# First mixers of a deep fp32 network on one core: gate projections moved last, raw copies of them, stick-breaking on every turn, output projection begun inside the attention

## The reference

```
def _token_mixer(h, w_in, w_out):
    proj = h @ w_in
    ...
    rq, rk, rv, rg, dq, dk, dv, sq, sk, sv = jnp.split(proj, points, axis=-1)
    ...
    y_ret = _retention(_rotate(_split_heads(rq, RET_HEADS), ret_freq),
                       _rotate(_split_heads(rk, RET_HEADS), ret_freq),
                       _split_heads(rv, RET_HEADS), rg)
    y_dil = _merge_heads(_dilated_attention(_rotate(_split_heads(dq, DIL_HEADS), rope_freq),
                                            _rotate(_split_heads(dk, DIL_HEADS), rope_freq),
                                            _split_heads(dv, DIL_HEADS)))
    y_sb = _merge_heads(_stick_breaking(_split_heads(sq, SB_HEADS), _split_heads(sk, SB_HEADS),
                                        _split_heads(sv, SB_HEADS)))
    y = jnp.concatenate([y_ret, y_dil, y_sb], -1).astype(h.dtype)
    return y @ w_out
...
def _retention(q, k, v, g):
    ...
    o = (o - mu) * lax.rsqrt(var + GN_EPS)
    return jax.nn.silu(g.astype(jnp.float32)) * _merge_heads(o)
...
def _stick_breaking(q, k, v):
        ...
        z = jnp.einsum('bhqd,bhsd->bhqs', q_blk, kf)
        log_beta = jax.nn.log_sigmoid(z)
        log_keep = jnp.where(causal, jax.nn.log_sigmoid(-z), 0.0)
        between = lax.cumsum(log_keep, axis=3, reverse=True) - log_keep
        a = jnp.where(causal, jnp.exp(log_beta + between), 0.0)
        return jnp.einsum('bhqs,bhsd->bhqd', a, vf)
```

## Time and profile before

| | us |
|---|---|
| median of 3 runs (3520.35 to 3524.16) | 3522.71 |
| profiled execution, span | 3520.2 |
| PE busy | 3433.7 (98%) |
| DVE busy | 1894.9 (54%) |
| ACT busy | 1198.5 (34%) |
| POOL busy | 519.9 (15%) |

### The profile page before, as it was taken

How to read it: one execution, slowest core, us unless ns; L and a number is a source line. 1 busy time by engine, 2 the same in 40 slices (tenths; PEclk the granted TensorE clock), 3 DMA queues, 4 the chain that set the end, 5 groups by cost and what they waited for, 6 DMA issues and landing times. The chain is left out here.

```text
span 3520.2 us, 40510 instructions
## 1 busy us (share of the span) xinstructions
PE 3433.7 (98%) x16478; PEld 2789.2 (79%) x16478; DVE 1894.9 (54%) x3227; ACT 1198.5 (34%) x1646; POOL 519.9 (15%) x454
## 2 busy tenths in 40 slices
PE   8999999999999999999999999989999999999999
PEld 5888876688888888876788877757888888878887
DVE  5555753664556455744752346885643345564433
ACT  3222352442224222453442234445432222352221
POOL 1010231210012010231210021112011110211111
PEclk9999999999999999999999999979999999999999
DMA  6444221133442444211132212101222222322221
GB/s 264 178 180 179 92 77 60 49 144 144 168 144 108 155 156 161 93 58 48 63 142 96 96 66 84 60 13 61 73 96 96 96 96 99 108 73 96 96 96 72
DMA packets 53036, 372.53 MB, mean 106 GB/s; under 512 B 6001, under 2 KB 6129, under 8 KB 10098
## 3 DMA queue, kind: packets, MB, share of 16 engines
q1 hardware_dynamic: 52850, 369.94, 28.8%
HBM read 367.82 MB, written 2.10 MB: 105 GB/s over the span
## 5 line engine op out<-in xcount | busy, mean ns | idle before, releaser
L1487 PE MATMUL ps<-s_hh,s_wh 128*128 128x512 f32 x2552 | 1012.8, 397 | 18.8 <-POOL s_hl L2691 14.1
L1487 PE MATMUL ps<-s_hh,s_wl 128*128 128x512 f32 x2552 | 998.3, 391 | 0.0
L1487 PE MATMUL ps<-s_hl,s_wh 128*128 128x512 f32 x2552 | 998.0, 391 | 0.0
L2137 DVE TENSOR_TENSOR s_wl<-s_stage,s_wh 128x2048 fp32r<-128x2048 f32 (+1 forms) x276 | 623.5, 2259 | 635.3 <-ACT s_wh L1814 635.3
L1814 ACT ACTIVATE s_wh<-s_stage 128x2048 fp32r<-128x2048 f32 (+1 forms) x276 | 519.2, 1881 | 586.0 <-PE ps L1487 427.0
L1487 PEld LDWEIGHTS ps<-s_hh,s_wh 128*128 128x128 f32 x2552 | 481.7, 189 | 138.9 <-issue 34.9
L1487 PEld LDWEIGHTS ps<-s_hh,s_wl 128*128 128x128 f32 x2552 | 481.7, 189 | 102.7
L1487 PE MATMUL ps<-s_ah,s_wh 128*128 128x512 f32 x1408 | 561.9, 399 | 0.7 <-POOL s_al L2730 0.7
L1487 PEld LDWEIGHTS ps<-s_hl,s_wh 128*128 128x128 f32 x2552 | 482.5, 189 | 98.0 <-issue 0.7
L1487 PE MATMUL ps<-s_ah,s_wl 128*128 128x512 f32 x1408 | 550.1, 391 | 0.0
L1487 PE MATMUL ps<-s_al,s_wh 128*128 128x512 f32 x1408 | 549.5, 390 | 0.0
(11 more groups left out here) (502 smaller groups left out, 3614.7 us busy)
## 6 DMA issues: line engine op xcount, KB each, us to landing
s_stage<-in_w_ada SPq DMA_DIRECT2D x64, 1024.0 KB, 4.8
s_stage<-in_ffn_w_gate SPq DMA_DIRECT2D x44, 1024.0 KB, 4.8
s_stage<-in_ffn_w_up SPq DMA_DIRECT2D x44, 1024.0 KB, 4.8
s_stage<-in_ffn_down SPq DMA_DIRECT2D x32, 1024.0 KB, 4.8
s_stage<-in_w_up SPq DMA_DIRECT2D x32, 1024.0 KB, 4.7
s_stage<-in_down_m SPq DMA_DIRECT2D x32, 1024.0 KB, 4.7
s_stage<-in_w_in SPq DMA_DIRECT2D x24, 1024.0 KB, 4.8
s_stage<-in_ffn_down SPq DMA_DIRECT2D x16, 768.0 KB, 4.3
```

Of the source, the lines that this page charges most:

```text
L1487: return pe.matmul(out, lhs, rhs, start=start, stop=stop, skip_group_check=True)
L2137: ins = dve.tensor_tensor(m.wl(ws)[:, a:z], m.STAGE[:, j % NS, a:z], m.wh(ws)[:, a:z].bitcast(F32), ALU.subtract)
```

## The change

It moves work within both mixers and leaves every product as it was.

- **Gates last.** The gate chunks 4 and 5 are projected behind dv. Their 8 groups run beside the dilated units, which before ran alone. The last product of a pair of dilated heads waits (`hold`) until all four gates are projected.
- **Raw copies.** `m_gate` copies the gate from PSUM to `rg`. `m_silu` applies Silu in place later, when all four gates are copied and all sixteen dilated exponentials (`weighed`) are in ACT's list.
- **Stick-breaking on every turn.** `pace = 2` is gone and `depth` is 5. The four tiles of `rg`, free until the gates come, serve as further scratch (`xg`), and later those of `rq` and `rk` (`xr`) serve the dilated units.
- **Output projection.** The order is (6, 7, 4, 5, 0, 1, 2, 3). Tiles are split when they are there (`ready`, `parted`), the first group (tiles 6 and 7) is put among the dilated units, and what is left of these runs from `pipeline` inside `project_out`. `m_part` of the retention's tiles is called in `ret_norm`.
- **Smaller things.** The first w_out chunk takes no chunk of w_ada along, so these move by one place in the following stages; `m_center` waits for its own previous result; ACT has 8 table loads where it had 16.

```
+            if ready:
+                self.until(lambda: ready(ks[i]) and ready(ks[i + 1]))
...
-            ch = self.take(name, idx0 + c, ada=c == 0)
-            tiles = (self.feat2(ch, kt, x, ver, True, order=order) if per == 2 and c == 0 else
+            ch = self.take(name, idx0 + c, ada=c == 0 and not ready)
+            tiles = (self.feat2(ch, kt, x, ver, True, order=order, ready=ready) if per == 2 and c == 0 else
                      (self.feat(ch, kt, nc, t, x, ver) for t in range(per)))
             for t, (b, pid) in enumerate(tiles):
+                if extra:
+                    self.pipeline()
+                    self.tmp.ids = [i for i in self.tmp.ids if i not in extra]
+                    self.burst, self.depth, extra = 1, 6, ()
...
+            while len(gated) < 4 or len(weighed) < 16:
+                yield
             for h in range(4):
-                b = self.banks.take()
-                self.add("ret_out", l, h, y, b)
-                self.banks.free(b, ("ret.out", l, h))
-                yield
+                self.add("m_silu", l, h)
+            yield
+            for h in range(5):
+                if h < 4:
+                    b = self.banks.take()
+                    self.add("ret_out", l, h, y, b)
+                    self.banks.free(b, ("ret.out", l, h))
+                if h:
+                    self.add("m_part", l, h - 1, (h - 1) % 2, self.hv, self.hfree)
+                    parted.append(h - 1)
+                if h % 2:
+                    yield
...
-        def setpace(n):
-            self.pace = n
+        def used_up():
+            for i in used:
+                self.tmp.after[i] = [("ret.s", l, h, 3) for h in range(4)]
+            self.tmp.ids += used
+            self.burst, self.depth = 2, 9
             return True
...
-        for i in extra:
+        for i in extra + unused:
             self.tmp.after[i] = [free]
-        self.tmp.ids += extra
+        self.tmp.ids += extra + unused
         tproj(11, "sv", 0)
         self.bg.extend(sb_units())
-        self.pace = 2
+        self.depth = 5
         proj(0, "rq")
         proj(1, "rk")
         self.active += [roped("rq", "ret"), roped("rk", "ret")]
         tproj(2, "rv", 0)
         tproj(3, "rv", 256)
-        self.bg.append(lambda: setpace(1))
         self.bg.append(lambda: len(ropes) >= 2 and len(sb_done) == 2)
         self.bg.extend(ret_units())
+        self.tmp.ids = [i for i in self.tmp.ids if i not in unused]
+        proj(6, "dq")
+        proj(7, "dk")
+        self.active += [roped("dq", "dil"), roped("dk", "dil")]
+        tproj(8, "dv", 0)
+        self.hv += 1
+        self.bg.append(lambda: len(ropes) == 4 and len(out_done) == 4 and used_up())
+        self.bg.extend(dil_units())
         for c in range(2):
             ch = self.take("w_in", l * 12 + 4 + c, ada=False)
             for t in range(2):
+                n = 2 * c + t
                 b, pid = self.feat(ch, 8, 256, t, "h", hv, turn=False)
-                self.add("m_gate", l, 2 * c + t, pid, b)
-                self.banks.free(b, ("m.g", l, 2 * c + t))
+                self.until(lambda: ("xg", n) not in self.tmp.busy)
+                self.add("m_gate", l, n, pid, b, self.tmp.after[("xg", n)])
+                self.banks.free(b, ("m.raw", l, n))
+                self.hfree = ("proj", pid)
+                gated.append(n)
                 self.tick()
             self.release(ch, ("proj", pid))
-        proj(6, "dq")
-        proj(7, "dk")
-        self.active += [roped("dq", "dil"), roped("dk", "dil")]
-        self.hfree = tproj(8, "dv", 0)
-        self.hv += 1
-        self.burst, self.depth = 2, 8
-        self.bg.append(lambda: len(ropes) == 4)
-        self.pipeline(dil_units())
-        self.burst, self.depth = 1, 6
-        order = (6, 7, 0, 1, 2, 3, 4, 5)
-        for i, n in enumerate(order[:6]):
+        for i, n in enumerate((6, 7)):
             self.add("m_part", l, n, i % 2, self.hv, self.hfree)
-        self.tmp.ids = [i for i in self.tmp.ids if i not in extra]
+        parted += [6, 7]
         gate = self.gate(l, 5, 1.0)
-        norm = self.project_out("w_out", l * 4, 8, 256, "h", self.hv, gate, "ln", order,
-                                (l, 1, (l, 6, 7), None))
+        norm = self.project_out("w_out", l * 4, 8, 256, "h", self.hv, gate, "ln", (6, 7, 4, 5, 0, 1, 2, 3),
+                                (l, 1, (l, 6, 7), None), None, lambda n: n in parted, extra + used)
...
+        if weighed is not None:
+            weighed.append(u)
...
+        while last and hold and not hold():
+            yield
...
-    def m_gate(l, h, pid, b):
-        e.wait_ge(("proj", pid))
-        act.activation(m.t["rg"][:, h, :], m.bank(b), ACT.Silu).then_inc(*e.up("act_evict", "m.g", l, h))
+    def m_gate(l, h, pid, b, free):
+        e.wait_ge(("proj", pid), free)
+        copy(m.t["rg"][:, h, :], m.bank(b)).then_inc(*e.up("act_evict", "m.raw", l, h))
+
+    def m_silu(l, h):
+        g = m.t["rg"][:, h, :]
+        e.wait_ge(("m.raw", l, h))
+        act.activation(g, g, ACT.Silu).then_inc(*e.up("act_gate", "m.g", l, h))
...
-        e.wait_ge(("m.v", l, "rv", c0, i))
+        e.wait_ge(("m.v", l, "rv", c0, i), ("m.c", l, c0, 0) if i else ("m.c", l, 0, 2) if c0 else None)
...
+        for k in range(4):
+            self.extra["xg", k] = self.t["rg"][:, k, :]
+        for k in range(4):
+            self.extra["xr", k] = self.t["rq" if k < 2 else "rk"][:, k % 2, :]
```

More of the change, by code:

```diff
@@ L324, in feat, with feat2 @@
         return b, self.pid
-    def feat2(self, ch, kt, x, ver, eager=False, n=S, order=None):
+    def feat2(self, ch, kt, x, ver, eager=False, n=S, order=None, ready=None):
         if not eager:
@@ L330, in feat2 @@
             return
-        yield from self.rest_of(*self.begin(ch, kt, n, x, ver, order))
+        yield from self.rest_of(*self.begin(ch, kt, n, x, ver, order), ready)
     def begin(self, ch, kt, n, x, ver, order=None, wide=(P, P)):
@@ L336, in begin, with rest_of @@
         return ch, self.pid - 1, kt, n, bs, x, ver, list(order or range(kt)), wide
-    def rest_of(self, ch, pid, kt, n, bs, x, ver, ks, wide):
+    def rest_of(self, ch, pid, kt, n, bs, x, ver, ks, wide, ready=None):
         for i in range(0, kt, 2):
+            if ready:
+                self.until(lambda: ready(ks[i]) and ready(ks[i + 1]))
             self.add("mm2", pid, ch, kt, n, bs, x, ver, ks, wide, i, i + 2)
@@ L625, in ffn, with project_out @@
         return after or (total if mean != "rms" else self.squares(*total))
-    def project_out(self, name, idx0, kt, nc, x, ver, gate, mean, order=None, nxt=None, raw=None):
+    def project_out(self, name, idx0, kt, nc, x, ver, gate, mean, order=None, nxt=None, raw=None, ready=None, extra=()):
         total, done, per = (self.new(), []), [], nc // P
@@ L676, in first_mixer @@
         extra = [("xm", i) for i in range(3)]
-        nk_done, sb_done, out_done, ropes = {}, [], {}, []
+        used = [("xr", i) for i in range(4)]
+        unused = [("xg", i) for i in range(4)]
+        sb_done, out_done, ropes, gated, parted, weighed = [], {}, [], [], [], []
         def proj(idx, key):
@@ L805, in dil_units @@
                     for c in range(2):
-                        yield self.attend("dil", l, 2 * pr + c, i, (i + 1) * P, cell, i == 3 and c == 1)
+                        yield self.attend("dil", l, 2 * pr + c, i, (i + 1) * P, cell, i == 3 and c == 1,
+                                          hold=lambda: len(gated) == 4, done=parted, weighed=weighed)
         one, two, free = self.late(norm, (("w_in", l * 12 + 9), ("w_in", l * 12 + 10)))
@@ L831, in first_mixer, with attend @@
             for t in range(2):
+                n = 2 * c + t
                 b, pid = self.feat(ch, 8, 256, t, "h", hv, turn=False)
-                self.add("m_gate", l, 2 * c + t, pid, b)
-                self.banks.free(b, ("m.g", l, 2 * c + t))
+                self.until(lambda: ("xg", n) not in self.tmp.busy)
[3 more added lines that the diff above has]
+                gated.append(n)
                 self.tick()
             self.release(ch, ("proj", pid))
-        proj(6, "dq")
-        proj(7, "dk")
-        self.active += [roped("dq", "dil"), roped("dk", "dil")]
-        self.hfree = tproj(8, "dv", 0)
-        self.hv += 1
-        self.burst, self.depth = 2, 8
-        self.bg.append(lambda: len(ropes) == 4)
-        self.pipeline(dil_units())
-        self.burst, self.depth = 1, 6
-        order = (6, 7, 0, 1, 2, 3, 4, 5)
-        for i, n in enumerate(order[:6]):
+        for i, n in enumerate((6, 7)):
             self.add("m_part", l, n, i % 2, self.hv, self.hfree)
-        self.tmp.ids = [i for i in self.tmp.ids if i not in extra]
+        parted += [6, 7]
         gate = self.gate(l, 5, 1.0)
-        norm = self.project_out("w_out", l * 4, 8, 256, "h", self.hv, gate, "ln", order,
-                                (l, 1, (l, 6, 7), None))
```

(6 more changed lines are left out.)

2 lines of the change are left out of this document (1 added, 1 removed).

## The result

The kernel after takes 3533.94 us (median of 5 runs, 3530.7 to 3536.97) against 3522.71 before; the ratio is 1.0033 with a 95% interval of 1.0022 to 1.0044. So it is slower by some 11 us. The forecast was 3525.9, within 0.2% as the likeliest, and the range 3506 to 3541 holds the result, just above the forecast case's own range (3517 to 3532), where the text expected only the slow rivals. Neither of them is what happened, as the stages show.

A forecast was written before the change was run, and what follows sets the result against it. PE bounds the kernel, busy 3433.7 of 3520.2 us. Mixer 1: -6.65 + 4.7 + 1.4 = -0.6; mixer 2: -3.25 + 4.7 + 2.3 = +3.8; together +3.2, span 3523.4, with 2.5 for the median 3525.9; range 3506 to 3541.

The forecast's parts named there:

- forecast case: Whole kernel: the summed terms, 3525.9 us, own range 3517 to 3532, chance 0.45.
- slow rivals: Mixers: retention tiles too late, about 3537 us, or an overlap that fails, about 3535; chance 0.28 together.
- The rest at nothing: Outside the mixers: moved w_ada chunk, added m_center wait and untouched stages cost nothing, bound 1 us either way.
- the one for stick-breaking: Stick-breaking on every turn, both mixers: PE waits on ACT's and DVE's queues, loss 3.3 to 6.1 us each, middle 4.7.
- Rival (1): Faster: slack hides stick-breaking at zero price, tail at its low end; -8.4 to -14 us, about 3508; chance 0.27.
- the other five waits of the forecast: PE in stick-breaking, per mixer: 0.6 and 0.6 us in the first pair, 0.3, 1.5 and 1.0 in the second.
- The gate and square waits: PE in both mixers: 2.05 us go by gates without Silu, 1.2 by earlier squares on ACT; -3.25 us each.
- The estimate of 21 us for eight: ACT: eight table loads fewer at about 2.66 us each by the skill page; not counted in the forecast.
- The tail: Dilated part beside gates, up to tile 5: 59.1 to 61.2 us, middle +1.4 in mixer 1, +2.3 in mixer 2.
- The clock: PE in mixer 1: two half-clock stretches behind gaps go, 1.7 us each, -3.4 us; none claimed in mixer 2.
- retention tiles too late: Output projection: POOL's products and low parts miss PE's groups, +4 us per mixer, about 3537; chance 0.28 with the other slow one.
- an overlap that fails: Dilated part beside gates: over a quarter left after the last gate matmul, +9 us, about 3535; shares the 0.28 chance.

The follow-up runs named there:

- a_ada1: Kernel after with the w_ada chunk taken along with the second w_out chunk in both mixers, where it was left out: 3524.68 us, 1.0002 to the kernel before.
- b_pace1b: Kernel before with stick-breaking on every turn, depth 5, no further scratch tiles, and the m_center wait this order needs: 3516.6 us, 0.9978.
- b_raw: Kernel before with gates copied raw and the four Silu done in place ahead of the retention's last products: 3522.7 us, 0.9996.
- a_part: a_ada1 with the high and low parts of tiles 6 and 7 listed right behind the fourth raw gate copy: 3517.19 us, 0.9981.
- a_defer: a_part with the second w_out chunk's split moved behind the last dilated steps and seven short DVE modulation steps ahead of the gates: 3509.56 us, 0.9959.
- a_defer_silu: a_defer with Silu and its table load two turns later, behind four copies of turned weights: 3504.51 us, 0.994 to the kernel before.
- b_noada: Kernel before with no w_ada chunk taken along with w_out in the mixers: 3539.08 us, 1.0043.
- experiment 3: Test of table loads around Silu on the kernel before, by b_raw (3522.7 us), with a count of the POOL step's lengths in all ten profiles.

## Why the prediction came out as it did

**The sign and the place were wrong at one step.** "The rest at nothing" said that the w_ada chunk is the same transfer and the same DVE work one place later, where PE has no gaps. The work is the same, and PE had indeed no gaps there; both are beside the point. What counts is the distance between DVE's rows and PE's column sum, and with the rows one place later the gate leaves one output tile between them. The term was two waits of 3.54 us and what the clock adds, 9.3 us by a_ada1, and the bound of 1 us had no row to rest on. I had counted the moved rows and not followed them to their consumer. That the range holds the result all the same is luck: this term was 9 us too low, and the one for stick-breaking, below, 7 us too high in waits.

**Stick-breaking: mechanism found, price wrong.** The walk through ACT's and DVE's queues held: the low part was forecast to end at 474.5 and ended at 473.66. DVE after, and PE's wait:

```profile
471.37 2.29 DVE L2171 TENSOR_TENSOR s_wl<-s_stage,s_wh 128x2048 fp32r<-128x2048 f32 x1 [4.03 <-ACT s_wh L1843]
473.58 0.75 DVE L2377 TENSOR_TENSOR s_rg<-s_rg,ps 128x256 f32<-128x256 f32 x2
474.24 0.68 DVE L2369 SCALAR_TENSOR_TENSOR s_nk<-ps,s_tmp 128x512 f32<-128x512 f32 x1
474.96 0.69 DVE L2371 TENSOR_TENSOR s_tmp<-ps,s_nk 128x512 f32<-128x512 f32 x1
475.57 0.68 DVE L2369 SCALAR_TENSOR_TENSOR s_nk<-ps,s_tmp 128x512 f32<-128x512 f32 x1
```

```profile
475.70 0.91 PE L1516 MATMUL ps<-s_nk,s_cc 128*128 128x384 f32 x2 [0.55 <-DVE s_tmp L2371]
```

The row is the sum of the third block's second head, which takes the bank that DVE's first two steps of the fourth block free. That bank came free at 475.65, not 476.6, and PE came to it at 475.15, not 474.5, so it waits 0.55 us, not 2.1. The bank that the next projection takes came free at 476.97, not 477.9, and PE starts there at 477.02 without a wait. Two queues that were each up to 1 us off make the whole difference. Of the other five waits of the forecast two are there, 0.16 and 0.46, in all 1.2 us per mixer against 4.7. Rival (1), that the slack hides it, was nearer, and even it did not have b_pace1b's gain.

**The gate and square waits: right in size, wrong in cause.** Both went (2.05 and 1.2 in each mixer). b_raw shows that the raw copies have no share in the first; b_pace1b shows that stick-breaking on every turn, with its depth, removes it alone, and most of the wait for the squares too (1.2 to 0.4). Four of the sixteen table loads went in b_raw, and nothing measurable came of it. The estimate of 21 us for eight, from the Trainium skill's page "ScalarE: Activation LUTs", section "What ACT_TABLE_LOAD costs", was rightly set aside in the text: by that page each switch takes 2.66 us, four of them 10.6 us as an estimate. The load itself agrees with it (1.28 us in the traces), while the drain does not show: Silu starts 0.02 us behind the load at 636.35. And b_raw, whose interval ends 4.6 us below the kernel before, shows that four fewer do not come off the time where PE does not wait for them.

**The tail: the chain right, the price and PE's waits not quite.** The output projection was forecast to begin 7.1 us behind the last gate matmul and began at 628.01, 7.7 us behind (620.3). The end of Silu was forecast at 17.9 and came at 19.5, tile 5 between 26.2 and 28.3 and at 27.8. From the first gate matmul to tile 5 it took 61.3 and 62.1 us against 59.1 to 61.2, so against the sums for the kernel before (58.8 and 57.9) the term is +2.5 and +4.2 where +1.4 and +2.3 were forecast. PE's waits in it were 4.89 us before the first matmul (5.5 forecast) and 3.66 + 0.45 before tile 5, where 8 to 10 behind POOL or DVE were forecast: the long one is for ACT's copy behind Silu, which the forecast did not have on PE's path. What it did not see either is that the length was a matter of order. The Trainium skill (page "Perfetto Trace Analysis", section "Optimizing Scalar/DVE Operations") suggests breaking up instructions that cause such bubbles, which no run here tried. Moving one 1.9 us split and its 2.29 us low part behind the chain, with seven short DVE steps ahead of it, gave 7.6 us from a_part to a_defer.

**The clock.** Forecast were 3.4 us saved in mixer 1. There 10.3 us at half clock went away (17.1 to 6.8 us), worth up to 5.1 us, but mixer 2 got 6.9 us more, and a stretch followed the wait at 1836:

```profile
1665.60:1672.40 6.80, 4.61 (x11) 3.67 (x12) 5.32 (x13) 3.02 (x5) 1.27 (x1) 0.50 0.08 10
...
1839.70:1843.00 3.30, 3.03 (x10) 2.57 (x11) 2.64 (x8) 0.00 (x0) 0.00 (x0) 0.50 0.97 353
```

The rivals on the slow side, retention tiles too late and an overlap that fails, did not happen: no wait stands between tiles 0 and 3, and a quarter of the dilated part was left at the last gate matmul as planned.

## What to carry to other kernels

When a step leaves its place, follow not only the work but the rule that says when its consumer is listed: a sum that is written when a gate asks for it becomes a wait as soon as its rows are made one step later. On a kernel whose one engine is 98% busy, look for the few long instructions (weight splits, a table load with its Silu) that stand in order ahead of short ones on a chain; moving them behind gave 20 us here, from a_ada1 to a_defer_silu, some 12 of them waits, where the change with its w_ada chunk put back gave nothing (1.0002). And do not name the cause of a wait by what stands next to it: an edit that removed the suspected cause alone changed nothing.

## What the runs showed of the hardware

The time at half clock differs between kernels in stages whose instructions are the same. The second layers took 1326.0 us before (58.0 us at half clock), 1324.6 after (58.0), and 1322.0 to 1322.2 in a_defer, a_defer_silu and b_pace1b (47.8). In b_noada mixer 2 lost 6.3 us in this way with no wait of its own that was new. It differs between executions of one kernel too: the kernel before had a mean granted clock of 0.987 in executions of 3518 to 3519 us and of 0.984 in one of 3529, with most at 0.985 or 0.986. A profile shows one execution. So of a difference of 5 us between two profiles of this kernel, all may be clock, and only the waits, counted one by one, and the medians of many runs tell a mechanism.

In the mixers the stretches at half clock stand at PE's waits. In mixer 1 of the kernel before all five begin within 2 us of the end of a wait of 1.2 to 2.65 us, after both stand at the waits of 4.89 and 3.66 us, and in mixer 1 of a_defer_silu, where no wait is over 1.6 us, there is none. But not every wait brings one: in mixer 2 of the kernel before, waits of 2.05 and 2.64 us have none, and the same waits in mixer 1 do. No run was made to settle what decides it.

A short POOL step beside a long DVE one can take five times as long: 2.43 us against 0.46 for 128x128, beside 2.28 us of a 128x2048 low part (experiment 3).
